# Recurrence gates of a hybrid encoder: six full products in a row, or three pairs of half-row products spread over the next work

## The reference

```python
xc, new_buf = causal_dwconv(x_a, conv_buf, conv_w)          # 4 taps
xb = xf.reshape(bsz, t, LRU_HEADS, LRU_BLOCK)                # 8 heads of 64 channels
r = sigmoid(einsum('bthi,hij->bthj', xb, w_a) + b_a)         # gate r
i = sigmoid(einsum('bthi,hij->bthj', xb, w_x) + b_x)         # gate i
log_a = -LRU_C * r * softplus(-lam)
a = exp(log_a)
gated_x = sqrt(-expm1(2.0 * log_a)) * (i * xf)
h = associative_scan(combine, (a, gated_x)) + a_cum * h0
y_a = h * silu(g_a)
```

## Time and profile before

| what | value |
|---|---|
| time, median of 3 runs | 1355.31 us (1355.01 to 1356.58) |
| the profiled execution: its own span | 1354.8 us |
| instructions | 27409 |
| PE busy | 1325.8 us, 98% of the span |
| DVE busy | 855.6 us, 63% |
| ACT busy | 434.6 us, 32% |
| POOL busy | 331.1 us, 24% |
| mean granted TensorE clock | 0.997 of full speed |

### The profile page before, as it was taken

The page is one execution under the profiler, slowest core; times in us unless marked ns, Lnnn a source line. Parts: engine busy times, 40 slices in busy tenths (PEclk is TensorE's granted clock), DMA queues, the critical chain, the costliest instruction groups (busy, mean ns, idle before and its releaser), DMA issues.

```text
span 1354.8 us, 27409 instructions
## 1 busy us (share of the span) xinstructions
PE 1325.8 (98%) x11200; PEld 904.0 (67%) x11200; DVE 855.6 (63%) x1939; ACT 434.6 (32%) x1044; POOL 331.1 (24%) x450
## 2 busy tenths in 40 slices
PE   5999999999999999999999999999999999999997
PEld 3577776666654454667877788877788777875543
DVE  3847874355454375785886858858578586782246
ACT  3213443344431233521422414224143241432221
POOL 1023200010013232523312423224222242212352
PEclk9999999999999999999999999999999999999999
DMA  9531016002034522121212112121121211440124
GB/s 356 235 75 36 5 36 271 8 1 79 3 130 167 195 85 108 13 81 19 71 46 68 34 34 83 38 77 40 34 83 29 75 50 34 127 159 26 35 94 168
DMA packets 63297, 111.96 MB, mean 83 GB/s; under 512 B 34778, under 2 KB 38690, under 8 KB 61618
## 3 DMA queue, kind: packets, MB, share of 16 engines
q1 hardware_dynamic: 63172, 110.21, 24.2%
HBM read 91.79 MB, written 18.40 MB: 81 GB/s over the span
## 4 chain that ended last, share of the span: by engine, by line
PE 88%; DVE 7%; POOL 1%; DMA 1%; issue 1%; ACT 1%; SPq 0%; DVEq 0%; POOLq 0%; ACTq 0%
PE psum L1132 83%; PE psum L1135 5%; DVE mem L2963 1%; DVE mem L2774 1%; DVE mem L3288 1%; DMA mem<-x_dram 1%; DVE mem L3054 0%; DMA y<-mem 0%; DVE mem L3165 0%; DVE mem L2943 0%; DMA mem<-x 0%; POOL mem L954 0%; DVE mem L2780 0%; ACT mem L1915 0%; ACT mem L2087 0%
## 5 line engine op out<-in xcount | busy, mean ns | idle before, releaser
L1132 PE MATMUL psum<-mem 32*32 32x32 f32 (+12 forms) x10592 | 1264.1, 304 | 4.9 <-DVE mem L2475 1.5
L1132 PEld LDWEIGHTS psum<-mem 128*128 128x128 f32 (+4 forms) x10592 | 835.7, 143 | 401.7 <-issue 217.0
L2963 DVE SCALAR_TENSOR_TENSOR mem<-mem 128x576 f32<-128x576 f32 (+1 forms) x126 | 106.1, 842 | 0.0
L1135 PE MATMUL psum<-mem 128*128 128x128 f32 (+1 forms) x608 | 85.1, 278 | 17.2 <-ACT mem L1927 12.9
L1135 PEld LDWEIGHTS psum<-mem 128*128 128x128 f32 (+1 forms) x608 | 70.7, 144 | 41.4 <-issue 21.0
L2278 ACT ACTIVATE mem<-mem 128x128 f32<-128x128 f32 x72 | 22.0, 305 | 127.6 <-DVE mem L3213 74.4
L2164 ACT ACTIVATE mem<-psum 128x288 f32<-128x288 f32 x28 | 11.4, 407 | 104.0 <-PE psum L1132 104.0
L1011 POOL COPY mem<-mem 128x3 f32<-128x3 f32 x24 | 8.4, 348 | 148.9 <-DVE mem L2921 70.1
L2056 ACT ACTIVATE mem<-mem 128x256 f32<-128x256 f32 x72 | 35.5, 495 | 26.4 <-DVE mem L2697 26.4
L2744 DVE TENSOR_TENSOR mem<-mem,psum 128x512 f32<-128x512 f32 x28 | 19.1, 684 | 37.4 <-PE psum L1132 37.0
L2174 ACT ACTIVATE mem<-mem 128x576 f32<-128x576 f32 (+1 forms) x42 | 32.7, 779 | 28.0 <-DVE mem L2941 28.0
(11 more groups left out here) (260 smaller groups left out, 1277.2 us busy)
## 6 DMA issues: line engine op xcount, KB each, us to landing
mem<-modw SPq DMA_DIRECT2D x12, 2048.0 KB, 12.2
mem<-w SPq DMA_DIRECT2D x44, 512.0 KB, 4.3
mem<-x SPq DMA_DIRECT2D x10, 512.0 KB, 4.7
x_dram<-mem SPq DMA_DIRECT2D x9, 512.0 KB, 2.9
mem<-row_dram SPq DMA_DIRECT2D x8, 576.0 KB, 5.2
mem<-x_dram SPq DMA_DIRECT2D x9, 512.0 KB, 3.7
mem<-wout SPq DMA_DIRECT2D x1, 4096.0 KB, 15.0
mem<-gs SPq DMA_DIRECT2D x8, 512.0 KB, 3.6
```

Source lines behind the costliest of these rows:

```text
L1132: return pe.matmul(*a, **k)
L1135: return pe.transpose(out, in_, ident[0:n, 0:n])
L2963: x = dve.scalar_tensor_tensor(cvm, U1[:, m, lo + j:hi + j], CW[:, 3 * g + ORDER[m], j:j + 1], cvm, ALU.mult, ALU.add)
```

## The change

Each gate product now has 64 rows and 128 columns: the weights of one head for both gates side by side. The two heads use rows 0 to 63 and rows 64 to 127 of PE, one product each, issued one behind the other, the first into bank 6, the second into bank 7. A part n is such a pair of products for one third of the tokens; three parts make the gates of a block. The upper head's weights are loaded with the two gates exchanged, so that each bank holds one gate in its lower and the other in its upper partitions.

ACT evicts each part with four activations of 64 partitions by 384 columns; for gate i they read one half of the partitions and write the other. It waits for `l_a` and `l_y` of the block in front before the first eviction of a block.

The parts are spread out: part 0 stands where the burst stood, part 1 behind the first half step of the next pair, and part 2 behind its second half step. In the last block, parts 1 and 2 stand behind the first and the second group of eight products. SP loads the gate weights with three transfers for each block where it used one. The semaphore counts follow: 3 for each block on `l_mm`, 12 on `lz_ev`.

```diff
-                sp.dma_start(gw, I["gw"][m]).then_inc(sem("gw_in"), 16)
+                lo, hi = slice(0, HD), slice(HD, P)
+                sp.dma_start(gw[lo], I["gw"][m, lo, :, lo]).then_inc(sem("gw_in"), 16)
+                for i in range(2):
+                    sp.dma_start(gw[hi, i], I["gw"][m, hi, 1 - i, hi]).then_inc(sem("gw_in"), 16)
...
                 for j in range(2):
                     freed(j, 0, "u4")
                     part("1", j, w1, 0, HT, 0, lo(j))
+                    between(j)
...
-                for i in range(6):
-                    if m or i >= 2:
-                        pe.wait_ge(sem("lz_ev"), 6 * m + i - 1)
-                    mm(B(6 + i % 2)[:, 0:NC], gw[:, i // 3], xc[:, (i % 3) * NC:(i % 3 + 1) * NC],
-                       start=True, stop=True).then_inc(sem("l_mm"), 1)
+                def part(n):
+
+                    if m or n:
+                        pe.wait_ge(sem("lz_ev"), 12 * m + 4 * n)
+                    for q in range(2):
+                        r = slice(q * HD, q * HD + HD)
+                        i = mm(B(6 + q)[:, 0:NC], gw[r].rearrange("p g c -> p (g c)"),
+                               xc[r, n * NC:(n + 1) * NC], start=True, stop=True)
+                    i.then_inc(sem("l_mm"), 1)
+
+                part(0)
                 if m < LM - 1:
-                    pair(m + 1)
+                    pair(m + 1, lambda j: part(j + 1))
                     return
...
-                for i in range(6):
-                    wait(act, sem("l_mm"), 6 * m + i + 1)
-                    if m and i == 0:
-                        wait(act, sem("l_a"), m)
-                    elif m and i == 3:
-                        wait(act, sem("l_y"), m)
-                    dst = (tr, ti)[i // 3][:, (i % 3) * NC:(i % 3 + 1) * NC]
-                    act.activation(dst, B(6 + i % 2)[:, 0:NC], ACT.Tanh, scale=0.5,
-                                   bias=gbias[:, m, i // 3:i // 3 + 1]).then_inc(sem("lz_ev"), 1)
-                wait(act, sem("lz_ev"), 6 * m + 3)
+                if m:
+                    wait(act, sem("l_a"), m)
+                    wait(act, sem("l_y"), m)
+                for n in range(3):
+                    wait(act, sem("l_mm"), 3 * m + n + 1)
+                    for i, dst in enumerate((tr, ti)):
+                        for q in range(2):
+                            r, s = (slice(x * HD, x * HD + HD) for x in (q, q ^ i))
+                            act.activation(dst[r, n * NC:(n + 1) * NC], B(6 + q)[s, 0:NC], ACT.Tanh, scale=0.5,
+                                           bias=gbias[r, m, i:i + 1]).then_inc(sem("lz_ev"), 1)
+                wait(act, sem("lz_ev"), 12 * m + 10)
```

More of the change, by code:

```diff
@@ L375, in encoder @@
         cb0 = take(LM, 1 + NS, PRE)
-        gw = take(2, P)
+        gw = take(2, HD)
         cv_at = at[0]
@@ L1240, in project, with pair @@
                     i.then_inc(sem(sname), 1)
-            def pair(p):
+            def pair(p, between=lambda j: None):
                 w1, w2 = PAIR_W[p]
@@ L1290, in gates @@
             def gates(m):
-                pe.wait_ge(sem("gw_in"), 16 * m + 16)
+                pe.wait_ge(sem("gw_in"), 48 * m + 48)
                 pe.wait_ge(sem("xc_ready"), m + 1)
@@ L1294, in gates, with last_free @@
                     pe.wait_ge(sem("mod_done"), 1)
-                for i in range(6):
-                    if m or i >= 2:
-                        pe.wait_ge(sem("lz_ev"), 6 * m + i - 1)
-                    mm(B(6 + i % 2)[:, 0:NC], gw[:, i // 3], xc[:, (i % 3) * NC:(i % 3 + 1) * NC],
-                       start=True, stop=True).then_inc(sem("l_mm"), 1)
+                def part(n):
[7 more added lines that the diff above has]
+                part(0)
                 if m < LM - 1:
-                    pair(m + 1)
+                    pair(m + 1, lambda j: part(j + 1))
                     return
+                def last_free(q, n):
+                    if q == 0 and n:
+                        part(n)
+                    pe.wait_ge(sem("st_add"), STEPS * (PAIRS - 1) + LAST_FREE[3 * q + n])
                 for q in range(2):
                     pe.wait_ge(sem(f"w0_in{q}"), 16 * m + 48)
-                    project(m, q, "g_mm", lambda n: pe.wait_ge(
-                        sem("st_add"), STEPS * (PAIRS - 1) + LAST_FREE[3 * q + n]))
+                    project(m, q, "g_mm", lambda n: last_free(q, n))
             tiles(LM, gates)
@@ L1419, in att @@
                 if first:
-                    pe.wait_ge(sem("lz_ev"), 6 * LM)
+                    pe.wait_ge(sem("lz_ev"), 12 * LM)
                 if sample:
@@ L2565, in conv0 @@
                 if m:
-                    dve.wait_ge(sem("l_mm"), 6 * m)
+                    dve.wait_ge(sem("l_mm"), 3 * m)
                     c.sync()
@@ L2597, in chain @@
                 dve.wait_ge(sem("l_a"), m + 1)
-                dve.wait_ge(sem("lz_ev"), 6 * m + 6)
+                dve.wait_ge(sem("lz_ev"), 12 * m + 12)
                 dve.wait_ge(sem("xc_ready"), m + 1)
```

2 lines of the change are left out of this document (1 added, 1 removed).

## The result

| kernel | median us | runs | ratio to before, 95% interval |
|---|---|---|---|
| before | 1355.16 (1354.97 to 1356.58) | 4 | |
| changed | 1376.45 (1375.07 to 1377.35) | 4 | 1.0152 [1.0139, 1.0165] |

The change makes the kernel 21.3 us slower. The forecast of 1365.8 us had the direction right and half the size; 1376.45 lies above its range of 1359 to 1370.

What follows compares the result with a forecast made beforehand. It took PE, busy 98% of the span, as the bound, with the `l_y` ring becoming longer than PE's way; 7.7 + 1.3 (POOL) + 1.5 (clock) = 10.5 us slower gave 1365.8 us, range 1359 to 1370.

Steps and rivals of the forecast that it cites:

- my 1.03: On PE, one part's pair of half products with switching was to cost 1.03 us; three parts 3.1 against 4.46.
- The ring: `l_y` end through ACT's evictions and PE's parts to the next DVE chain: 37.3 us a turn against PE's 30.3.
- its 7.7: Blocks 0 to 3: sum of the delay up to the end of the last projection's groups, +7.7 us.
- In block 3 a group of 5.16 us lies between the parts; part 1 starts at 215.29: Block 3 on PE: part 1 was to start only 0.5 us late, behind one group of the last projection.
- The eviction term: On ACT, twelve evictions replace six; each was to last 0.58 us and the next start 0.48 behind it.
- The clock term: PE's clock may fall to 1.2 GHz after the waits of 5.5 and 7 us: +1.5 us, bounds 0 and +5.9.
- POOL's term: POOL's sums meet DVE's scans behind a chain's start and hold them up: +1.3 us, bounds -4.9 and +2.7.
- the first rival: POOL's sums do not hold up DVE's scans, so chains are as short as chain 2: 1359.1 us, chance 0.16.
- PE alone would gain 1.35 us at each of four blocks: Products on PE: three parts take 3.1 us against the burst's 4.46, 5.4 us gained in all.

Runs made afterwards that it cites:

- e7_groups: The changed kernel with the last projection's six groups in the order 3, 0, 1, 2, 4, 5; 1372.06 us, ratio 1.0123.
- e5_halves: The changed kernel with each part's evictions ordered lower, lower, upper, upper, each from the half it writes (gate i not computed rightly); 1373.65 us, one run.
- e14_split_evictions: The kernel before, full products in one burst, with every eviction split into two of 64 partitions; 1363.40 us, ratio 1.0058.
- e6_pool_later: The changed kernel with POOL's sums for pairs 2 and 3 starting only behind c11 of the pair in front; 1377.91 us, ratio 1.0169.
- e4_full_spread: The kernel before with its six full products spread, two at each part's place, evictions and `l_y` wait as before; 1362.63 us, ratio 1.0052.
- e9_wait_first: The kernel before with only ACT's wait for `l_y` moved to the first of its six evictions; 1359.03 us, ratio 1.0025.
- e8: The kernel before with full products spread, ACT making `la` and `lw_` ahead of its last two evictions, DVE waiting later for gate i; 1353.63 us, ratio 0.9985.
- e12: The changed kernel with `lh` in its own rows, last groups reordered, `la` and `lw_` in thirds and evictions reordered; 1365.62 us, ratio 1.0072.
- e1: The changed kernel with `lh` of blocks 0 to 2 in free rows of YT, so no eviction waits for `l_y`; 1371.88 us, ratio 1.0115.
- e10: The changed kernel with ACT's wait for `l_y` moved from the first to the third eviction of a block; 1372.95 us, ratio 1.0127.

## Why the prediction was wrong, step by step

**What held.** Two half products run side by side: part 0 starts at 103.46 and the next full product at 104.30, so a part costs 0.85 us, less than my 1.03. The ring closes as described: ACT's first eviction is released by line 2667 in all three blocks, and PE's waits for it are visible. Their split was off, since PE first waits for c11: by the loads' record 3.1 and then 3.5 us at part 1 in block 1 (5.5 forecast), 4.0 and 3.5 in block 2 (7.0 forecast). What lies behind the stretch is just shifted.

**The ledger.** From the first start of block 0's products to the last eviction of the six groups: 105.08 to 235.59 before, 103.46 to 255.38 now, 130.5 and 151.9 us, 21.4 more, where the terms gave 7.7 + 1.3 + 1.5 = 10.5. The way that the prediction added up to its 7.7, piece by piece:

| piece | forecast | measured | more |
|---|---|---|---|
| products of block 0 to chain 0 | 11.61 | 12.84 | 1.2 |
| chain 0 and chain 1, to the end of `l_y` | 25.18, 26.66 | 26.43, 27.39 | 2.0 |
| chain 2 | 23.46 | 23.46 | 0 |
| end of `l_y` 0 to chain 1 | 10.60 | 13.14 | 2.5 |
| end of `l_y` 1 to chain 2 | 10.60 | 11.90 | 1.3 |
| end of `l_y` 2 to part 1's eviction, block 3 | 3.05 | 9.73 | 6.7 |
| the rest | | | 0 |

It adds up to 13.7 us above the 7.7, which closes the account at 21.4. The waits for c11 are in none of the pieces: they lie ahead of part 1, which waits for ACT anyway.

**The step that failed most: "In block 3 a group of 5.16 us lies between the parts; part 1 starts at 215.29".** I traced the moved order of evictions into ACT's queue, but not the delayed DVE chain into PE's other waits. The first group of the last projection writes the bank that c12 frees, c12 stands behind `l_y` 2 in DVE's order, and `l_y` 2 ended at 218.62. The forecast's own times would have told it: with `l_y` 2 at 213.19 and c12 some 0.7 us behind, the group could not begin before 214, where it had to begin at 215.29 - 5.16 = 210.1. PE waited 3.98 us for it, and the group then took 8.25 us instead of 5.16, most of it at half clock. e7_groups takes exactly this away and wins 6.2 us there. Of the 6.7 us in the table 3.1 are clock and 0.4 evictions, so 3.2 are left for the wait for c12, which the prediction had put at nothing.

**The eviction term was mis-sized.** "One lasts 0.58 us and the next starts 0.48 behind it": I read 0.48 from evictions that all began at partition 0, and they go at 0.60 us when the half read or written changes from one to the next. The way from the products to the chain has ten such distances, 10 x 0.12 = 1.2 us in block 0; each of two turns of the ring has ten as well (1.3 us measured in block 2), and the last piece has three, 0.4 us: 4.2 us in all. e5_halves shows the distance, e14_split_evictions that it holds in a burst as well.

**The clock term was too small.** I took 1.5 with bounds of 0 and 5.9. 1.2 us in block 1 (part to part 4.63 and not 3.40) and 3.1 in block 3 (8.25 and not 5.16) make 4.3. The stretch at 26 us had shown it; I reckoned its aftermath to be short. Together evictions 4.2, clock 4.3, scans 2.0 and the wait for c12 3.2 make the 13.7; only the last is what was left over. Against what the forecast had for them (0, 1.5, 1.3 and 0) they are 10.9 us more, the whole miss in the trace.

**POOL's term, "I take +1.3".** Its cause was right and its size nearly: +2.0, chains 0 and 1 being held up by POOL during their small scans. The Trainium skill, in SBUF — State Buffer, section Who interferes with whom, says that a DVE instruction with two SBUF inputs contends with a GpSimd instruction that reads SBUF. The trace agrees, with 4.32 us for the scans beside POOL and 1.25 alone. Its lower half of the range (the first rival, 1359.1) is refuted. What e6_pool_later adds is that avoiding the collision at the scans brings nothing by itself.

**A sentence that was wrong in principle: "PE alone would gain 1.35 us at each of four blocks".** True of PE, but the change hands the gates to the chain later, and e4_full_spread shows that this alone costs 7 us in a kernel whose PE is busy for 98%: a busy PE still has queued waits for DVE, and their slack is limited. In the kernel before c11 is there at 123.4 us and PE's step 4 begins, by an estimate from the pair's start at 109.56 and 40 products of 0.485 us, at 129.0: 5.6 us of slack. The bank for the first group is free at 200.6 and the group begins at 204.4: 3.8 us. The later chain (3.2 us) with its scans beside POOL (3.2 us more) uses that up. The prediction counted the late chain only inside the `l_y` ring. Of the ring itself, e9_wait_first says 3.4 us.

Not tried: the change with the clock held up, which no edit of mine could do without taking the waits away too; so the clock's share is read from the traces alone.

## What to carry to other kernels

Before shortening the work of a saturated engine, write down when its products' *last consumer* may start, and follow that delay through every queue that it feeds: here 3 us later on DVE, which became 6 in the collision with POOL, cost 7 us on PE, and giving them back (e8) made the same placement no loss and perhaps a small gain. Reading a result out in more pieces of fewer partitions costs by their number here (0.58 us each, whole or half), and a price per piece is good only for pieces that start at the same partitions as those it was read from. And where a wait moves ahead in a queue, look for the first thing behind it that does not need it.

## What the runs showed of the hardware

- Activations of 64 partitions by 384 columns from PSUM start 0.48 us apart where the half read and the half written stay (e5), and 0.59 to 0.61 where either or both change (e5, e12, e14). Whole ones of 128 partitions follow each other after 0.45 (e8).
- Eight scans of 16 columns take 1.25 us alone, and 4.31 to 4.45 us while POOL adds tiles of 128 x 512 (the change, e1, e4, e5, e7, e10, e12). POOL's first such sum, beside the long scan ahead of them, takes 2.47 us in block 0 of the change and 3.34 in block 1, and one takes 1.26 alone.
- A pair of half-row products of 384 columns, with its loads and the change back to full products, takes 0.85 us up to the next full product, and a full product takes 0.645.
- By the products' record, waits of PE of 2.1 us (e9), 2.5 (e4), 2.7 to 4.0 (the change) and 4.4 (e6) were followed by 3.4 to 6.8 us at 1.2 GHz; one of 3.0 in the change, ending at 185.8, and one of 3.6 in e1, ending at 167.7, were not. The waits of before in the same stretch, 0.7 us at most in the loads' record, were followed by none.
